# Modulation columns of a two-block transformer layer: partition sums by 32x32 transposes on VectorE instead of small matmuls, and the blocks moved one pair up

## The reference, cut to what matters

```
def first_block(...):
    h = _rms_norm(x, attn_norm);  x = x + _hybrid_mixer(h, w_in, ..., w_out)
    h = _rms_norm(x, ffn_norm);   x = x + (silu(h @ w_gate) * (h @ w_up)) @ w_down   # D_FF = 5632

def second_block(...):
    c_act = silu(c)                                   # 2048 numbers
    mod = c_act @ ada_w + ada_b                       # 2048 x 12288
    sh1, sc1, g1, sh2, sc2, g2 = split(mod, 6)
    h = rms_norm(x, mix_pre_g) * (1 + sc1) + sh1
    x = x + g1 * rms_norm(hybrid_mixer(h, ...), mix_post_g)
    h = rms_norm(x, ffn_pre_g) * (1 + sc2) + sh2
    x = x + g2 * rms_norm(swiglu_ffn(h, ...), ffn_post_g)
```

## Time and profile before

| | before |
|---|---|
| median of 3 runs | 2306.86 us (2304.01 to 2308.09) |
| profiled execution: time / span in the trace | 2309.19 us / 2307.1 us |
| PE busy | 2262.2 us, 98% |
| DVE busy | 1514.5 us, 66% |
| ACT busy | 1086.2 us, 47% |
| POOL busy | 173.2 us, 8% |
| granted TensorE clock, mean | 0.992 |
| HBM read | 508.04 MB, 221 GB/s over the span |

### The profile page before, as it was taken

One profiled execution on the slowest core, in us unless ns is written; L12 is line 12 of the kernel. 1 busy time (PEld: TensorE's weight loads), 2 busy tenths in 40 slices (PEclk: granted clock), 3 DMA queues, 4 the chain that ended last, 5 costly groups with the idle time before them and its releaser, 6 DMA issues.

```text
span 2307.1 us, 29343 instructions
## 1 busy us (share of the span) xinstructions
PE 2262.2 (98%) x10352; PEld 1868.1 (81%) x10352; DVE 1514.5 (66%) x1952; ACT 1086.2 (47%) x1515; POOL 173.2 (8%) x193
## 2 busy tenths in 40 slices
PE   9999999999999999999989999989999999999998
PEld 7888877888888888888868887777888888888886
DVE  6555377767777777777766886776777544554555
ACT  6555464544444444344345776654443344444444
POOL 4000100000000000000001885000000000000000
PEclk9999999999999999999989999999999999999999
DMA  7566517688888888888766664676887666666664
GB/s 232 178 182 189 160 47 288 223 266 280 277 281 286 277 276 280 282 279 277 266 200 191 192 183 127 214 260 188 283 277 264 190 190 188 191 191 192 191 189 147
DMA packets 274503, 511.79 MB, mean 222 GB/s; under 512 B 20071, under 2 KB 28949, under 8 KB 274124
## 3 DMA queue, kind: packets, MB, share of 16 engines
q1 hardware_dynamic: 270252, 509.94, 69.6%
q10 hardware_dynamic: 4128, 0.26, 0.1%
HBM read 508.04 MB, written 2.10 MB: 221 GB/s over the span
## 4 chain that ended last, share of the span: by engine, by line
PE 93%; DVE 3%; issue 2%; DMA 1%; ACT 1%; SPq 0%; DVEq 0%; ACTq 0%
PE bank L945 30%; PE bank L961 28%; PE bank L962 28%; PE bank L916 1%; PE bank L1018 1%; DMA raw<-in_w_out 1%; PE bank L1091 1%; PE bank L930 1%; DVE ada_acc L1784 1%; PE bank L1006 1%; DVE w_lo L1807 1%; ACT w_hi L1388 0%; PE bank L1059 0%; PE bank L1047 0%; PE bank L818 0%
## 5 line engine op out<-in xcount | busy, mean ns | idle before, releaser
L1807 DVE TENSOR_TENSOR w_lo<-raw,w_hi 128x1024 fp32r<-128x1024 f32 x760 | 936.9, 1236 | 593.8 <-ACT w_hi L1388 585.0
L1388 ACT ACTIVATE w_hi<-raw 128x1024 fp32r<-128x1024 f32 x760 | 802.4, 1059 | 978.8 <-PE bank L945 912.2
L961 PE MATMUL bank<-w_hi,act_hi 128*128 128x512 f32 x2016 | 792.2, 393 | 0.0
L962 PE MATMUL bank<-w_hi,act_lo 128*128 128x512 f32 x2016 | 786.0, 390 | 0.0
L945 PE MATMUL bank<-w_lo,act_hi 128*128 128x512 f32 x2080 | 558.9, 391 | 0.0
L945 PEld LDWEIGHTS bank<-w_lo,act_hi 128*128 128x128 f32 x2080 | 392.1, 189 | 82.6
L962 PEld LDWEIGHTS bank<-w_hi,act_lo 128*128 128x128 f32 x2016 | 379.2, 188 | 77.9 <-issue 0.7
L961 PEld LDWEIGHTS bank<-w_hi,act_hi 128*128 128x128 f32 x2016 | 379.1, 188 | 77.8 <-issue 0.7
L961 PE MATMUL bank<-w_hi,mid_hi 128*128 128x512 f32 x960 | 379.5, 395 | 6.8 <-ACT w_hi L1388 5.6
L962 PE MATMUL bank<-w_hi,mid_lo 128*128 128x512 f32 x960 | 374.7, 390 | 0.0
L1784 DVE SCALAR_TENSOR_TENSOR ada_acc<-ada_raw,c_act,ada_acc 128x512 f32<-128x512 f32 x360 | 269.7, 749 | 9.0 <-DMA ada_raw<-in_ada_w 1.9
(11 more groups left out here) (272 smaller groups left out, 1007.1 us busy)
## 6 DMA issues: line engine op xcount, KB each, us to landing
ada_raw<-in_ada_w SPq DMA_DIRECT2D x192, 512.0 KB, 5.2
raw<-in_w_gate SPq DMA_DIRECT2D x176, 512.0 KB, 4.4
raw<-in_w_up SPq DMA_DIRECT2D x176, 512.0 KB, 4.4
raw<-in_w_down SPq DMA_DIRECT2D x176, 512.0 KB, 4.3
raw<-in_w_in SPq DMA_DIRECT2D x168, 512.0 KB, 3.8
raw<-in_w_out SPq DMA_DIRECT2D x64, 512.0 KB, 5.5
raw<-in_cmp_w_k SPq DMA_DIRECT2D x4, 512.0 KB, 4.5
raw<-in_cmp_w_v SPq DMA_DIRECT2D x4, 512.0 KB, 4.7
```

Source lines behind the costliest of these rows:

```text
L961: pe.matmul(A_[t][:, :], h_, w_hi[:, s, kk, :], start=(k == 0), stop=False)
L962: pe.matmul(A_[t][:, :], l_, w_hi[:, s, kk, :], start=False, stop=False)
L1388: act.activation(w_hi[:, U % SPLIT_SLOTS].rearrange("p k n -> p (k n)"), raw[:, R % RAW_SLOTS].rearrange("p k n -> p (k n)"), ACT.Copy).th ...
L1807: dve.tensor_tensor(w_lo[:, U % SPLIT_SLOTS].rearrange("p k n -> p (k n)"), raw[:, R % RAW_SLOTS].rearrange("p k n -> p (k n)"), w_hi[:, U ...
```

## The change

**Sums.** For column blocks the four small matmuls (L1006) and the copy (L1792) go. In their place DVE does two operations after the last step of the block: it transposes each 32x32 square of `ada_acc` within itself into `ada_t` (128x512), and sums groups of 32 along the free side, 128x512 to 128x16, into `col_part`. What is left to sum is over the four groups of 32 partitions. That is done for 8 blocks at once by one fp32 matmul of 128x128 with a constant matrix `quads`, which POOL makes: the first at unit 2 of `MOD_AT` (the first chunk of `w_down` in the second group of `S_FFN1`), the second at unit 2 of `S_IN2[1]`. At unit 7 of the same chunks DVE copies the result into `mod_cols` (four copies) and builds `norm_shift` and `norm_scale` for one half (`mods`). No chunk of `S_FFN1` now waits on DVE for a sum of PE for column blocks.

**Place.** The list of `S_FFN1` is now `col_blocks` without the leading `None`: each block sits one pair earlier, the first pair of gate and up chunks has one and the last pair of `w_down` has none. In the first chunk the four steps are at units 2, 3, 4 and 5 (`ADA_FIRST`); `ADA_LAST` is gone. Nothing of the modulation stands between `S_FFN1` and `S_IN2` any more. Waits that counted blocks now count rows and columns apart.

```diff
-    ADA_LAST = (0, 1, 2, 4)
+    ADA_FIRST = (2, 3, 4, 5)
...
-    S_FFN1, LAST_FFN1 = ffn("", "x", [None] + col_blocks, 0, LAST_OUT1)
-
-    KEEP_FFN1 = pending.pop()
+    S_FFN1, LAST_FFN1 = ffn("", "x", col_blocks, 0, LAST_OUT1)
+
+    assert not pending
+    N_MOD = n_col[0] // 2
+    MOD_AT = next(c for c in S_FFN1 if "loop" not in c and c["ada"] and c["ada"]["row"] >= N_MOD)
...
+            link(pool.memset(quads[:, :], 0.0))
+            for a in range(4):
+                ins = pool.affine_select(out=quads[:, :], in_=quads[:, :], pattern=[[0, 4], [-1, 32]],
+                                         compare_op=ALU.not_equal, fill=1.0, base=-32 * a, channel_multiplier=1)
...
-                        if a["kind"] == "col":
-                            for j in range(4):
-                                ins = pe.matmul(MISC[0][:, j:j + 1], ada_acc[:, j * P:(j + 1) * P], ones[:, 0:1],
-                                                start=True, stop=True)
...
+                    if u == 2 and (c is MOD_AT or c is S_IN2[1]):
+                        half = 0 if c is MOD_AT else 1
+                        w_cols = N_MOD * CW // 32
+                        pe.wait_ge(quads_made, 1)
+                        pe.wait_ge(ada_out, 2)
+                        pe.wait_ge(ada_cols, (half + 1) * N_MOD)
+                        pe.matmul(MISC[0][:, 0:w_cols], quads[:, :], col_part[:, half * w_cols:(half + 1) * w_cols],
+                                  start=True, stop=True).then_inc(mods_summed, 1)
...
                     if k == 0:
-                        if a["blk"] >= 1:
-                            dve.wait_ge(ada_summed, at(a["blk"], r, 1))
+                        if a["kind"] == "col":
+                            dve.wait_ge(ada_summed, 2)
...
+                if a["kind"] == "col" and a["half"] == 1 and i == 3:
+                    dve.wait_ge(ada_used, at(2 * unit + 2, r, 16))
+                    dve.transpose(ada_t[:, :], ada_acc[:, :]).then_inc(ada_turned, 1)
+                    dve.wait_ge(ada_turned, at(a["row"] + 1, r, 1))
+                    w_cols = CW // 32
+                    dve.tensor_reduce(col_part[:, bass.ds(at(w_cols * a["row"], r, w_cols), w_cols)],
+                                      ada_t[:, :].rearrange("p (b i) -> p b i", i=32), AX.X, ALU.add).then_inc(
+                        ada_cols, 1)
...
+            def mods(half):
+
+                n = 2 * KD
+                dve.wait_ge(mods_summed, half + 1)
+                for q in range(4):
+                    ins = dve.tensor_copy(mod_cols[32 * q:32 * q + 32, half * n:(half + 1) * n],
+                                          MISC[0][32 * q:32 * q + 32, 0:4 * n].rearrange("p (n q) -> p n q", q=4)[:, :, q])
+                link(ins)
+                sh, sc = half * n, half * n + KD
+                dve.tensor_copy(norm_shift[:, 2 + half, :], mod_cols[:, sh:sh + KD])
+                link(dve.scalar_tensor_tensor(norm_scale[:, 2 + half, :], mod_cols[:, sc:sc + KD], 1.0,
+                                              cols[:, (2 + half) * KD:(3 + half) * KD], ALU.add, ALU.mult))
...
             mean_root(2)
-            ada_keep(KEEP_FFN1, None)
-            dve.wait_ge(ada_out, KEEP_FFN1["blk"] + 1)
-            for i in range(2):
-                sh, sc = 2 * i * KD, (2 * i + 1) * KD
-                dve.tensor_copy(norm_shift[:, 2 + i, :], mod_cols[:, sh:sh + KD])
-                link(dve.scalar_tensor_tensor(norm_scale[:, 2 + i, :], mod_cols[:, sc:sc + KD], 1.0,
-                                              cols[:, (2 + i) * KD:(3 + i) * KD], ALU.add, ALU.mult))
```

More of the change, by code:

```diff
@@ L69, in chunk @@
         if ada is not None and ada["half"] == 1:
-            pending.append(dict(kind=ada["kind"], dst=ada["dst"], blk=ada["blk"]))
+            pending.append(dict(kind=ada["kind"], dst=ada["dst"], row=ada["row"]))
         if ada is not None:
@@ L105, in build_two_blocks @@
     U_CMP = pos["U"]
-    ada_blk = [0]
+    ada_blk, n_row, n_col = [0], [0], [0]
     def ada_pair(kind, col, dst, step=0, n=1):
@@ L112, in ada_pair @@
         ada_blk[0] += n
-        return [dict(kind=kind, col=col, dst=dst, blk=b, half=h, step=step) for h in range(2)]
+        count = n_col if kind == "col" else n_row
+        i = count[0]
+        count[0] += n
+        return [dict(kind=kind, col=col, dst=dst, blk=b, row=i, half=h, step=step) for h in range(2)]
     def out_pairs(w, dst, prev, ada, first):
@@ L160, in pair @@
                         pos["A"] += 8 * (trips - 1)
-                        pending[0]["blk"] += trips - 1
+                        pending[0]["row"] += trips - 1
                         pending[0]["dst"] += (trips - 1) * (4 if a[0]["kind"] == "col" else CW)
@@ L449, in build_two_blocks @@
         Cs.close()
+        Es = ExitStack()
+        ada_t = sb("ada_t", [P, CW], F32, Es)
+        col_part = sb("col_part", [P, 2 * N_MOD * CW // 32], F32, Es)
+        quads = sb("quads", [P, P], F32, Es)
+        Es.close()
         Ds = ExitStack()
@@ L493, in build_two_blocks @@
         gate_loaded = sem("gate_loaded")
+        ada_turned, ada_cols, quads_made, mods_summed = (sem("ada_turned"), sem("ada_cols"), sem("quads_made"),
+                                                         sem("mods_summed"))
         blk_zero, blk_ready, cmp_used = sem("blk_zero"), sem("blk_ready"), sem("cmp_used")
@@ L648, in load @@
                         load_params(R - RAW_SLOTS)
-                    ada_at = ADA_LATE if c is S_OUT2[0] else ADA_LAST if c is S_FFN1[-1] else ADA_AT
+                    ada_at = ADA_LATE if c is S_OUT2[0] else ADA_FIRST if c is S_FFN1[0] else ADA_AT
                     if c["ada"] and u in ada_at:
                         ada_load(c, r, ada_at.index(u))
-                if c["ada"] and c["nu"] < 7 and c is not S_FFN1[-1]:
+                if c["ada"] and c["nu"] < 7:
                     ada_load(c, r, 3)
@@ L998, in gemm @@
                     a = c["ada"]
-                    if a and a["half"] == 1 and u == 5:
+                    if a and a["half"] == 1 and u == 5 and a["kind"] != "col":
                         pe.wait_ge(ada_used, at(2 * (a["A"] + 4), r, 16))
-                        if a["blk"] >= 1:
-                            pe.wait_ge(ada_out, at(a["blk"], r, 1))
-                        if a["kind"] == "col":
-                            for j in range(4):
-                                ins = pe.matmul(MISC[0][:, j:j + 1], ada_acc[:, j * P:(j + 1) * P], ones[:, 0:1],
-                                                start=True, stop=True)
-                        else:
-                            ins = pe.matmul(MISC[0][:, :], ones[:, :], ada_acc[:, :], start=True, stop=True)
-                        ins.then_inc(ada_summed, 1)
+                        if a["row"] >= 1:
+                            pe.wait_ge(ada_out, at(a["row"], r, 1))
+                        pe.matmul(MISC[0][:, :], ones[:, :], ada_acc[:, :], start=True, stop=True).then_inc(
+                            ada_summed, 1)
+                    if u == 2 and (c is MOD_AT or c is S_IN2[1]):
[6 more added lines that the diff above has]
+                                  start=True, stop=True).then_inc(mods_summed, 1)
             def scores(j, j0):
@@ L1777, in ada_step @@
                     if k == 0:
-                        if a["blk"] >= 1:
-                            dve.wait_ge(ada_summed, at(a["blk"], r, 1))
+                        if a["kind"] == "col":
+                            dve.wait_ge(ada_summed, 2)
+                        elif a["row"] >= 1:
+                            dve.wait_ge(ada_summed, at(a["row"], r, 1))
                         dve.wait_ge(ada_bias_loaded, at(16 * (a["blk"] + 1), r, 16))
@@ L1816, in split @@
                         ada_at = ADA_LATE
-                    if c is S_FFN1[-1]:
-                        ada_at = ADA_LAST
+                    if c is S_FFN1[0]:
+                        ada_at = ADA_FIRST
                     if c["ada"] and u in ada_at:
@@ L1822, in split @@
                         dve.wait_ge(gate_loaded, 16)
+                    if u == 7 and (c is MOD_AT or c is S_IN2[1]):
+                        mods(0 if c is MOD_AT else 1)
                     if u == 2 and c["keep"]:
@@ L1849, in split @@
                     return
-                if c["ada"] and nu < 7 and c is not S_FFN1[-1]:
+                if c["ada"] and nu < 7:
                     ada_step(c, r, 3)
@@ L2034, in _ @@
             ada_keep(KEEP_OUT2, None)
-            dve.wait_ge(ada_out, KEEP_OUT2["blk"] + 1)
+            dve.wait_ge(ada_out, KEEP_OUT2["row"] + 1)
             for t in range(TT):
```

15 lines of the change are left out of this document (8 added, 7 removed).

## The result

The changed kernel takes 2284.53 us (median of 4 runs, 2283.11 to 2286.46); the kernel before took 2305.82 us (4 runs, 2304.01 to 2308.09). The ratio is 0.9908 [0.9891, 0.9925], 21.3 us less. The forecast was 2286 us, 21.0 us less. The profiled execution took 2284.62 us, span 2282.8 us, 24.3 us less than the one before.

The account below looks back on a forecast made before the run. PE, busy 98% of the span, was taken to bound the kernel. Gains of 14.3 + 6.5 + 0.8 less 0.6 made 21.0 us, taking the median from 2306.86 to about 2286 us; range 2280.5 to 2293.

Parts of the forecast that it names:

- The 64 small matmuls: S_FFN1's column-block sums on PE: removing them gains 0.95 us at each of 15 places, 14.3 us.
- the tail: Last chunk of S_FFN1: without a block in the last pair its 22.83 us fall to 16.32, gaining 6.5 us.
- closing matmul: Two new fp32 matmuls on PE, each finishing the sums of eight blocks: 0.3 us each, 0.6 us lost.
- The rival that they cost less than their distance: Small matmuls in S_FFN1: PE runs into the next bound, gain only 6.7 us, 2300 us; chance 0.05.
- The rival that only half comes back: Last chunk of S_FFN1: ACT also waits for additions into x_res, so half of 6.5 us returns, 2289; chance 0.12.
- The gap: Between S_FFN1 and S_IN2: the last copy and building of the norms leave DVE's chain, gaining 0.8 us.
- Transpose and sum on DVE: After each column block's last step: 0.7 us each, 1.4 us a block, hidden by DVE's slack, cost 0.
- The limit: DVE in each block: beyond about 7.1 us for transpose and sum PE waits; DVE becomes the bound, about 2310, chance 0.04.
- The first pair: First chunk of S_FFN1, now with a block: act_lo about 4.1 us later yet in time by 0.6 us, cost 0.
- The rival did not happen: First chunk of S_FFN1: the block there makes PE wait, price 2 to 6.5 us, 2288 to 2292.5; chance 0.14.
- its own forecast of 2288.2: Whole kernel: the earlier profiled execution's 2309.19 us less the summed gain of 21.0 us.

Follow-up runs that it names:

- e6: Changed kernel with four small fp32 matmuls on constants put back at each of 16 places, result unused, nobody waiting: 2301.3 us.
- e2: Kernel before with only the blocks moved one pair up, small matmuls kept and norms still built in the gap: 2301.73 us.
- e1: Changed kernel's sums by transposes, but blocks in their old places, last pair with steps at units 0, 1, 2 and 4: 2290.95 us.
- e10: e1 with the last pair's modulation loads cut to a quarter of their bytes, all waits kept: 2290.53 us.
- e9: e1 with the last chunk's four steps at units 1, 2, 4 and 5 instead of 0, 1, 2 and 4: 2289.09 us.
- e3: Changed kernel with the four copies and two operations building the first half of the norms back in the gap before S_IN2: 2285.98 us.
- e5: Changed kernel with each block's DVE transpose done eleven times: 2317.23 us.
- e7: Changed kernel with the first chunk's steps at units 1, 2, 5 and 6 instead of 2 to 5: 2284.86 us.
- e4: Changed kernel with each block's DVE transpose done five times: 2287.38 us.
- e11: Changed kernel with row sums split on DVE into two fp32r matmuls one unit later, and mid_lo ahead of DVE's last step in one chunk: 2281.1 us.

## Why the prediction was right

**The 64 small matmuls.** Forecast 15 x 0.95 = 14.3 us. S_FFN1 lost 20.55; without the tail's 6.5 and with one closing matmul in it, that leaves 14.3. e6 gives 0.955 a block. The rival that they cost less than their distance is refuted: nothing else came to fill the places. That the price is that of the loads of stationary columns fits the trace of before, where PEld (the weight loads) begins a load every 0.11 us (from the second to the last of these eight, 523.23 to 523.89):

```profile
523.00 1.08 PEld L1006 LDWEIGHTS bank<-ones,ada_acc 128*128 128x128 f32 x8
```

**The tail.** Forecast 6.5, measured 6.5 (22.83 to 16.3 us), by the placement alone in e2. The mechanism, SP's loads held by DVE's steps, holds: the hold stands in e1's queue, and with a quarter of the bytes 4.4 of 5.5 us stay (e10). Two details of it did not: the spacing of the last chunk's steps, which the prediction had named with the cause, explains 1.6 of 5.5 us (e9), and about 1 us goes with the small matmuls, probably as DVE's wait for PE's sum, which the prediction had called off the path. The change takes away both, so the number did not suffer; that is luck as far as these details go. The rival that only half comes back is out.

**The gap.** Forecast 0.8. e3 shows that such work costs its full time there, and e2 divides it, 0.20 for the copy and 0.58 for the norms. PE's timeline in the gap, before and then after:

```profile
1194.57 1.22 PE L872 MATMUL bank<-ysb,ones 128*128 128x256 f32 x2 [2.12 <-DVE ysb L1567]
```

```profile
1174.47 0.70 PE L891 MATMUL bank<-ysb,ones 128*128 128x256 f32 x2 [1.34 <-DVE ysb L1589]
```

The wait for DVE is 2.12 - 1.34 = 0.78 us shorter, which is the forecast. The gap as a whole lost 1.30; the other 0.52 are the same two matmuls, 1.22 us long at a granted clock of 0.50 and 0.70 at 1.00. They are no gain of the change: in the repeat of the changed kernel they took 1.22 us again, at 0.50 and with the same wait of 1.34, and its gap is 8.44.

**The closing matmuls.** Forecast 0.3 each. PE's timeline at the second, and its records:

```profile
1211.84 0.38 PE L1031 MATMUL bank<-col_part,quads 128*128 128x128 f32 x2
1211.97 0.48 PE L980 MATMUL bank<-w_hi,act_hi 128*128 128x512 f32 x1
...
1214.83 0.39 PE L980 MATMUL bank<-w_hi,act_hi 128*128 128x512 f32 x1
```

```profile
L1031 PE MATMUL bank<-col_part,quads x4: 270/272/273, 891.7 to 1211.9; 128*128 128x128 f32 x4
```

The units beside it are 2.86 us each, 0.28 more in all. The record is that of the earlier trace rows to 3 ns: the nearest row by width was the right one, not the one by name.

**Transpose and sum on DVE.** Forecast 0.7 each and hidden. DVE's timeline in the same up chunk as the earlier trace rows:

```profile
564.74 0.71 DVE L1812 STREAM_TRANSPOSE ada_t<-ada_acc 128x512 f32<-128x512 f32 x1
565.60 0.69 DVE L1815 TENSOR_REDUCE col_part<-ada_t 128x512 f32 x1
566.20 2.58 DVE L1850 TENSOR_TENSOR w_lo<-raw,w_hi 128x1024 fp32r<-128x1024 f32 x2
570.28 1.23 DVE L1850 TENSOR_TENSOR w_lo<-raw,w_hi 128x1024 fp32r<-128x1024 f32 x1 [1.50 <-ACT w_hi L1410]
```

The work is caught up within two units: DVE waits 1.50 us for ACT again at 570.28. The limit was put at 7.1 us for both and 1.6 us of PE's wait at 8.7; e5 gave 1.35 us of wait and 1.63 in length at 9.0, so in a chunk of 8 units the limit lies nearer 7.6 (9.0 - 1.35). The Trainium skill, "VectorE: DVE Perf Modes", section "Rules for kernel authors", calls tensor_reduce the slowest operation of DVE. Here it was not: the sum took 0.69 us, the transpose of the same tile 0.71 and one addition into it 0.75. The prediction's estimate from the Trainium skill, the same page, section "The three transpose paths", 1.24 us for four pieces of 128 columns, is too high for this one operation of 512 columns in fp32: 0.71 us.

**The first pair.** Forecast 0, with 0.6 us of margin. DVE, then ACT, then PE of the first chunk (answers to the earlier trace rows):

```profile
445.39 1.28 DVE L1719 TENSOR_TENSOR x_res<-bank,x_res 128x512 f32<-128x512 f32 x2
...
456.35 0.87 DVE L1614 SCALAR_TENSOR_TENSOR act_lo<-bank,norm_scale,act_hi 128x256 fp32r<-128x256 f32 x2
```

```profile
446.71 0.63 ACT L1205 ACTIVATE ysb<-x_res 128x512 f32<-128x512 f32 x1 [4.40 <-DVE x_res L1719]
```

```profile
458.27 0.39 PE L980 MATMUL bank<-w_hi,act_hi 128*128 128x512 f32 x1
```

act_lo is ready at 457.22, PE wants it at 458.27: 1.05 us of margin. S_FFN1 started 1.23 us later in this execution, so against that start ACT's squares came 1.9 us later (forecast 2.2) and act_lo 3.7 us later (forecast 4.1). The step's working over three engines held to 0.4 us. The rival did not happen, and e7, with the steps at other units, costs nothing either.

**What the sum missed.** 2286 against 2284.53 in the medians is 1.5 us, under a thousandth. The profiled execution is 3.6 us below its own forecast of 2288.2; 3.0 of that is the clock in the attention stretch. The clock in and behind the gap gave another 0.5 and 1.4; the later start of S_FFN1 took 1.2 back and the rest of the table 0.5, 3.2 us in all, against 3.3 by the spans. PE's first matmuls of S_IN2 before and after, as stretches:

```profile
1198.20:1201.70 3.50, 3.49 (x8) 2.78 (x9) 3.49 (x6) 1.65 (x3) 0.00 (x0) 0.50 0.16 16
```

```profile
1177.60:1181.00 3.40, 3.40 (x9) 2.75 (x10) 3.40 (x6) 1.63 (x3) 0.00 (x0) 0.59 0.17 20
```

Before, S_IN2 began wholly at the lower level (0.50 is 1.2 GHz) and was back at the full level 6.0 us after its first matmul; in the changed kernel 2.8 us after it. That the chunk ahead now has no pause is not the reason: e3 and e4 have no pause there either and were back after 5.4 and 5.8 us, and e9, which has pauses, after 2.9. The runs leave open what sets it.

## What to carry to other kernels

When one engine is busy 98% of the time, price each of its small instructions by the distance of its neighbours' starts, against the same place without it, not by its one moving column; then look for the rest in the stretch where its units are longer than elsewhere. A queue that issues two kinds of loads in order holds the urgent kind back as long as the slots of the other kind are used up, so keep the second kind out of a stretch where the engine that frees its slots is itself held up. And work moved to an engine that runs ahead is free only up to its idle time plus its lead: compute both before, and test with multiples of the operation.

## What the runs showed of the hardware

- A transpose of 32x32 squares of 128x512 in fp32 takes 711 ns on DVE, about as long as a copy of that size from PSUM (682 ns), and eleven in a row 8.18 us. A copy within SBUF, with a change of type to fp32r, took 427 ns (e11).
- Four fp32 matmuls with one moving column cost 0.95 us, with two records each, about 0.12 us a record, where PEld begins a load every 0.11 us. One such matmul costs 0.24 us, hardly less than the closing matmul with 128 moving columns (0.28).
- A sum over partitions of 128x512 costs PE 0.90 us in fp32 and 0.45 us as a high and a low part in fp32r, at 0.43 + 0.69 us of DVE (measured by e11's casts and subtractions of the same width).
- After a wait of 1.35 us PE's unit was 1.63 us longer (e5), after one of 0.85 us 1.14 us longer (e4), both at full clock: a pause costs PE about 0.3 us beside the wait.
- The same 115 matmuls of the attention stretch took 3.0 us longer at a mean granted clock of 0.89 than at 1.00, and in 14 traces this stretch lasted from 26.8 to 29.8 us: a single profile cannot settle a difference of that size.
